# The head, the router and the tail of a two-layer decoder kernel: other load order, earlier router weights, fewer serial steps before the expert loop

## What is computed

```python
for layer in range(DEPTH):                      # 2
    h = rmsnorm(x, mix_norm[layer])
    z = h @ w_in[layer]                         # 1024 x 4392
    ...
    x = x + merged @ w_out[layer]
    h2 = rmsnorm(x, ffn_norm[layer])
    if layer % 2 == 0:
        x = x + swiglu(h2, dense_w1[i], dense_w3[i], dense_w2[i])
    else:
        x = x + moe_swiglu(h2, moe_router[i], moe_w1[i], moe_w3[i], moe_w2[i])

def moe_swiglu(h, w_router, w1, w3, w2):
    logits = einsum('bsd,de->bse', h, w_router)
    top_v, top_i = top_k(logits, 2); top_w = softmax(top_v)
    gate = sum(one_hot(top_i, 8) * top_w[..., None])
    for e in range(8):
        y = y + gate[..., e:e + 1] * swiglu(h, w1[e], w3[e], w2[e])   # hidden width 3584
```

## Time and profile before

| | us |
|---|---|
| median of 3 runs | 1618.19 (1617.88 to 1620.21) |
| the profiled execution, its own time | 1617.99 |
| its span, first to last instruction | 1616.2 |
| PE busy | 1549.6 (96%) |
| DVE busy | 1275.5 (79%) |
| ACT busy | 1052.8 (65%) |
| DMA queue q1, share of 16 engines | 80.6% |

### The profile page before, as it was taken

How to read it: one execution, slowest core, us unless ns; L and a number is a source line. 1 busy time by engine, 2 the same in 40 slices (tenths; PEclk the granted TensorE clock), 3 DMA queues, 4 the chain that set the end, 5 groups by cost and what they waited for, 6 DMA issues and landing times.

```text
span 1616.2 us, 23222 instructions
## 1 busy us (share of the span) xinstructions
PE 1549.6 (96%) x7253; PEld 1273.0 (79%) x7253; DVE 1275.5 (79%) x1358; ACT 1052.8 (65%) x1159; POOL 3.8 (0%) x9
## 2 busy tenths in 40 slices
PE   5999999999999679999999999999999999999997
PEld 4888888788888668878877877887887887887885
DVE  4785755446876569789789789889979979988978
ACT  5556544336565437677687687777768768768766
POOL 0000000000000000000000000000000000000000
PEclk8999999999999779999999999999999999999998
DMA  7553565257553649699999999989989989989985
GB/s 286 170 177 109 184 190 187 92 192 272 166 172 113 198 142 352 204 370 368 312 352 367 350 321 371 372 294 371 371 292 367 368 299 369 372 300 370 372 304 184
DMA packets 361357, 445.34 MB, mean 276 GB/s; under 512 B 17713, under 2 KB 272729, under 8 KB 361321
## 3 DMA queue, kind: packets, MB, share of 16 engines
q1 hardware_dynamic: 360840, 442.75, 80.6%
q0 software_dynamic: 480, 2.13, 0.4%
...
## 4 chain that ended last, share of the span: by engine, by line
PE 82%; issue 4%; DVE 4%; DMA 4%; ACT 3%; SPq 2%; DVEq 0%; ACTq 0%
PE bank L736 25%; PE bank L738 25%; PE bank L737 25%; DMA w_raw<-in_moe_w 3%; PE bank L1020 2%; ACT w_hi L447 2%; PE bank L1046 2%; DVE w_lo L1111 1%; SPq L353 1%; DVE hT_lo L1483 1%; PE bank L816 1%; DMA w_raw<-in_w_in 1%; PE bank L762 1%; ACT hT_hi L727 0%; PE bank L800 0%
## 5 line engine op out<-in xcount | busy, mean ns | idle before, releaser
L1111 DVE TENSOR_TENSOR w_lo<-w_raw,w_hi 128x1024 fp32r<-128x1024 f32 (+1 forms) x448 | 781.9, 1757 | 115.9 <-ACT w_hi L447 115.2
L447 ACT ACTIVATE w_hi<-w_raw 128x1024 fp32r<-128x1024 f32 (+1 forms) x448 | 664.1, 1492 | 160.7 <-PE bank L738 146.8
L736 PE MATMUL bank<-w_hi,hT_hi 128*128 128x512 f32 (+1 forms) x1424 | 567.6, 399 | 13.2 <-DVE hT_lo L1126 9.7
L738 PE MATMUL bank<-w_hi,hT_lo 128*128 128x512 f32 (+1 forms) x1424 | 555.1, 390 | 0.0
L737 PE MATMUL bank<-w_lo,hT_hi 128*128 128x512 f32 (+1 forms) x1424 | 553.9, 389 | 0.0
L736 PEld LDWEIGHTS bank<-w_hi,hT_hi 128*128 128x128 f32 x1424 | 269.0, 189 | 69.8 <-DVE hT_lo L1126 10.3
L738 PEld LDWEIGHTS bank<-w_hi,hT_lo 128*128 128x128 f32 x1424 | 268.5, 189 | 56.2
L737 PEld LDWEIGHTS bank<-w_lo,hT_hi 128*128 128x128 f32 x1424 | 269.3, 189 | 50.5
L441 ACT ACTIVATE w_hi<-w_raw 128x2048 fp32r<-128x2048 f32 (+2 forms) x100 | 169.7, 1699 | 180.2 <-PE bank L738 168.3
L1106 DVE TENSOR_TENSOR w_lo<-w_raw,w_hi 128x2048 fp32r<-128x2048 f32 (+2 forms) x100 | 201.7, 2020 | 106.7 <-ACT w_hi L441 105.5
L736 PE MATMUL bank<-w_hi,hiddenM_hi 128*128 128x512 f32 x448 | 178.8, 399 | 1.1
...
## 6 DMA issues: line engine op xcount, KB each, us to landing
...
```

Source lines behind the costliest of these rows:

```text
L447: act.activation(whi[:, m % SLOTS, 0:n], raw8[m % 8][:, 0:n], ACT.Copy).then_inc(s_hi, 1)
L736: pe.matmul(dst, ahi, bhi, start=start, stop=False)
L738: return pe.matmul(dst, alo, bhi, start=False, stop=stop)
L1111: dve.tensor_tensor(wlo[:, m % SLOTS, 0:n], raw8[m % 8][:, 0:n], whi[:, m % SLOTS, 0:n], ALU.subtract).then_inc(s_lo, 1)
```

## The change

- **Head.** SP issues the constants before `x` and then the weight chunks at once; the seven small loads are issued by ACT, the four gain rows with a semaphore of their own (`s_gn`). PE's gain matmul moves behind `x_T`, and its result is waited for at the second column block. ACT makes `hT_hi` quarters 0 and 1, splits chunk 0, makes quarters 2 and 3, then splits chunks 1 to 3; DVE likewise.
- **Router weights** are loaded by POOL at the start and split in the head, behind `norm(0)`.
- **Router.** PE takes the 48 router matmuls quarter by quarter as `hT_lo` appears, right behind `x_T(3, 1)`. `xs` is gone: ACT makes `xrhi` from `X` with the rms factor as scale, DVE makes `xrlo` in one instruction, now behind the masks. POOL clears `yhi`, `ylo` and `selT`, waited for behind `gather(0)`. `s_pos` is signalled after three matmuls. The gates move behind `gathered_lo(0)`, the overflow table is made in one pass over wider tiles. The split of the loop's fourth chunk (`ahead(c + 25)` in layer 1) moves on ACT behind `xrhi` and on DVE behind `gathered_lo(0)`.
- **Loads of the expert loop.** Chunk 7 waits for `s_ms` (norm(3)'s mean square) and not for `xrlo`.
- **Tail.** The output is stored in two DMAs of 0.5 MB, each after two of the last four `add_rows`.

The expert loop's own code is the same. SBUF addresses behind `norm_stats` shift, since the router weights have a place of their own.

```diff
+            sp.dma_start(cst[:], A["consts"]).then_inc(s_cst, 16)
             sp.dma_start(X[:], A["x"][0].rearrange("(t p) d -> p t d", p=P)).then_inc(s_x, 16)
-            sp.dma_start(cst[:], A["consts"]).then_inc(s_cst, 16)
-            for name, r, n in (("mix_norm", 0, 16), ("ffn_norm", 16, 16), ("pool_scale", 32, 8)):
-                sp.dma_start(prow[r:r + n, :], A[name].rearrange("l (k p) -> (l k) p", p=P)).then_inc(s_par, 16)
-            for j, name in enumerate(("q_norm", "k_norm")):
-                v = nrow[:].rearrange("o (l j d) -> o l j d", l=2, j=2)
-                for l in range(2):
-                    sp.dma_start(v[:, l, j], A[name][l:l + 1, :]).then_inc(s_par, 16)
...
                 elif m == 7:
-                    sp.wait_ge(s_xrl, 2)
+                    sp.wait_ge(s_ms, 4)
...
-            sp.wait_ge(m_xa, njobs * 4 + 4)
-            sp.dma_start(out[0].rearrange("(t p) d -> p t d", p=P), X[:]).then_inc(s_out, 16)
-            sp.wait_ge(s_out, 16)
+            for t in range(TT):
+                sp.wait_ge(m_xa, njobs * 4 + (2 * t + 2))
+                sp.dma_start(out[0, t * P:t * P + P, :], X[:, t, :]).then_inc(s_out, 16)
+            sp.wait_ge(s_out, 16 * TT)
...
+                if l == 0:
+                    pool.dma_start(wr[:], A["moe_router"][0].rearrange("(k p) e -> p k e", p=P)).then_inc(s_wrl, 16)
+            pool.wait_ge(s_rt, 1)
+            for z in (yhi, ylo, selT[:]):
+                ins = pool.memset(z.bitcast(F32), 0.0)
+            ins.then_inc(s_y0, 1)
 
 
         @block.scalar
...
-                ahead(c + 25)
+                if l == 0:
+                    ahead(c + 25)
                 hT_hi(3 * l + 2, 16 + 8 * l, (2, 3))
                 norm(2 * l + 1)
...
-            for c in range(LOOK):
+            for name, r, n in (("mix_norm", 0, 16), ("ffn_norm", 16, 16), ("pool_scale", 32, 8)):
+                act.dma_start(prow[r:r + n, :], A[name].rearrange("l (k p) -> (l k) p", p=P)).then_inc(s_par, 16)
+            for j, name in enumerate(("q_norm", "k_norm")):
+                v = nrow[:].rearrange("o (l j d) -> o l j d", l=2, j=2)
+                for l in range(2):
+                    act.dma_start(v[:, l, j], A[name][l:l + 1, :]).then_inc(s_gn, 16)
+            act.wait_ge(s_pcol, 1)
+            hT_hi(0, 0, (0, 1))
+            split(0, chunk_words(0))
+            hT_hi(0, 0, (2, 3))
+            for c in range(1, LOOK):
                 split(c, chunk_words(c))
-            act.wait_ge(s_x, 16)
-            act.wait_ge(s_pcol, 1)
-            hT_hi(0, 0)
             norm(0)
+            act.wait_ge(s_wrl, 16)
+            act.activation(wrhi[:], wr[:], ACT.Copy).then_inc(s_wrh, 1)
...
-            act.wait_ge(s_xs, TT)
+            act.wait_ge(s_rs, 4)
             for t in range(TT):
-                act.activation(xrhi[:, t, :], xs[:, t, :], ACT.Copy).then_inc(s_xr, 1)
+                act.activation(xrhi[:, t, :], X[:, t, :], ACT.Copy, scale=st[:, 3, t:t + 1]).then_inc(s_xr, 1)
+            ahead(LAYER1 + MIX_CHUNKS - 1)
             act.activation(identR[:], ident, ACT.Copy)
-            act.wait_ge(s_wrl, 16)
-            act.activation(wrhi[:], wr[:], ACT.Copy).then_inc(s_wrh, 1)
-            act.wait_ge(s_gd, 1)
-            act.activation(pr[:, 1, :], pr[:, 0, :], ACT.Exp).then_inc(s_ge, 1)
 
...
             gathered_hi(0)
+            act.wait_ge(s_gd, 1)
+            act.activation(pr[:, 1, :], pr[:, 0, :], ACT.Exp).then_inc(s_ge, 1)
...
-            pe.wait_ge(s_par, 7 * 16)
-            pe.transpose(bank[6][:, 0:40], prow[:], cst[0:40, C_ID:C_ID + 40])
-            pe.matmul(bank[7][:, 0:4 * HD], cst[0:1, C_ONE:C_ONE + P], nrow[:], start=True, stop=True).then_inc(s_prt, 1)
+            pe.wait_ge(s_par, 3 * 16)
+            pe.transpose(bank[6][:, 0:40], prow[:], cst[0:40, C_ID:C_ID + 40]).then_inc(s_prt, 1)
             pe.wait_ge(s_x, 16)
             x_T(0, 0)
             x_T(0, 1)
+            pe.wait_ge(s_gn, 4 * 16)
+            pe.matmul(bank[7][:, 0:4 * HD], cst[0:1, C_ONE:C_ONE + P], nrow[:], start=True, stop=True).then_inc(s_prt, 1)
             layer(0, 0)
 
...
-            pe.wait_ge(s_tlo, 24)
 
 
             pe.wait_ge(s_wrh, 2)
-            for t in range(TT):
-                for k in range(KC):
-                    ins = three(bank[4][:, t * E:t * E + E], hThi[:, k, t * P:t * P + P], hTlo[:, k, t * P:t * P + P],
-                                wrhi[:, k, :], wrlo[:, k, :], k == 0, k == KC - 1)
+            for j in range(4):
+                pe.wait_ge(s_tlo, 20 + j + 1)
+                for k in (2 * j, 2 * j + 1):
+                    for t in range(TT):
+                        ins = three(bank[4 + t][:, 0:E], hThi[:, k, t * P:t * P + P], hTlo[:, k, t * P:t * P + P],
+                                    wrhi[:, k, :], wrlo[:, k, :], k == 0, k == KC - 1)
             ins.then_inc(s_rt, 1)
             pe.wait_ge(s_mk, 1)
             tri, ones = cst[:, C_TRI:C_TRI + P], cst[:, C_ONE:C_ONE + P]
-            pe.matmul(bank[5][:, 0:E], tri, tmp8[:, 0, :], start=True, stop=True)
-            pe.matmul(bank[5][:, E:2 * E], tri, tmp8[:, 1, :], start=True, stop=False)
-            pe.matmul(bank[5][:, E:2 * E], ones, tmp8[:, 0, :], start=False, stop=True)
-            pe.matmul(bank[5][:, 2 * E:3 * E], ones, tmp8[:, 0, :], start=True, stop=False)
-            pe.matmul(bank[5][:, 2 * E:3 * E], ones, tmp8[:, 1, :], start=False, stop=True).then_inc(s_pos, 1)
+            pe.matmul(bank[6][:, 0:E], tri, tmp8[:, 0, :], start=True, stop=True)
+            pe.matmul(bank[6][:, E:2 * E], tri, tmp8[:, 1, :], start=True, stop=False)
+            pe.matmul(bank[6][:, E:2 * E], ones, tmp8[:, 0, :], start=False, stop=True).then_inc(s_pos, 1)
+            pe.matmul(bank[7][:, 0:E], ones, tmp8[:, 0, :], start=True, stop=False)
+            pe.matmul(bank[7][:, 0:E], ones, tmp8[:, 1, :], start=False, stop=True).then_inc(s_pos, 1)
...
             pe.wait_ge(s_xrl, 2)
+            gather(0)
             pe.wait_ge(s_y0, 1)
-            gather(0)
...
+            dve.wait_ge(s_pcol, 1)
+            hT_lo(0, 0, (0, 1))
+            split(0, chunk_words(0))
+            hT_lo(0, 0, (2, 3))
+            split(1, chunk_words(1))
+            dve.wait_ge(s_prt, 2)
             dve.tensor_copy(gain[:].rearrange("p l j d -> p (l j d)"), bank[7][:, 0:4 * HD]).then_inc(s_pcol, 1)
-            for c in range(LOOK):
+            for c in range(2, LOOK):
                 split(c, chunk_words(c))
             dve.wait_ge(s_pcol, 2)
-            hT_lo(0, 0)
             norm(0)
+            dve.wait_ge(s_wrh, 1)
+            dve.tensor_tensor(wrlo[:], wr[:], wrhi[:], ALU.subtract).then_inc(s_wrh, 1)
...
-                dve.tensor_scalar(xs[:, t, :], X[:, t, :], st[:, 3, t:t + 1], None, ALU.mult).then_inc(s_xs, 1)
-            dve.wait_ge(s_xs, TT)
+                ins = dve.tensor_scalar(lg[:, t, :], bank[4 + t][:, 0:E], st[:, 3, t:t + 1], None, ALU.mult)
+            chain(ins)
             for t in range(TT):
-                dve.wait_ge(s_xr, t + 1)
-                dve.tensor_tensor(xrlo[:, t, :], xs[:, t, :], xrhi[:, t, :], ALU.subtract).then_inc(s_xrl, 1)
-            dve.wait_ge(s_wrh, 1)
-            dve.tensor_tensor(wrlo[:], wr[:], wrhi[:], ALU.subtract).then_inc(s_wrh, 1)
-            dve.wait_ge(s_rt, 1)
-            for z in (yhi, ylo, selT[:]):
-                ins = dve.memset(z.bitcast(F32), 0.0)
-            ins.then_inc(s_y0, 1)
+                ins = dve.max(v8[:, t, :], lg[:, t, :])
+            chain(ins)
             for t in range(TT):
-                chain(dve.tensor_scalar(lg[:, t, :], bank[4][:, t * E:t * E + E], st[:, 3, t:t + 1], None, ALU.mult))
-            for t in range(TT):
-                chain(dve.max(v8[:, t, :], lg[:, t, :]))
-            for t in range(TT):
-                chain(dve.max_index(ix8[:, t, :], v8[:, t, :], lg[:, t, :]))
-            dve.tensor_tensor(pr[:, 0, :], v8[:, :, 1], v8[:, :, 0], ALU.subtract).then_inc(s_gd, 1)
+                ins = dve.max_index(ix8[:, t, :], v8[:, t, :], lg[:, t, :])
+            chain(ins)
             chain(dve.tensor_copy(ixf[:], ix8[:]))
             iota8 = cst[:, C_IOTA:C_IOTA + E]
             for t in range(TT):
                 dve.tensor_scalar(m0[:, t, :], iota8, ixf[:, t, 0:1], None, ALU.is_equal)
-                chain(dve.tensor_scalar(m1[:, t, :], iota8, ixf[:, t, 1:2], None, ALU.is_equal))
+                ins = dve.tensor_scalar(m1[:, t, :], iota8, ixf[:, t, 1:2], None, ALU.is_equal)
+            chain(ins)
             chain(dve.tensor_tensor(tmp8[:], m0[:], m1[:], ALU.add))
             dve.nop().then_inc(s_mk, 1)
-            dve.wait_ge(s_ge, 1)
-            chain(dve.tensor_scalar(pr[:, 2, :], pr[:, 1, :], 1.0, None, ALU.add))
-            chain(dve.reciprocal(pr[:, 2, :], pr[:, 2, :]))
-            chain(dve.tensor_tensor(pr[:, 3, :], pr[:, 1, :], pr[:, 2, :], ALU.mult))
             for t in range(TT):
```

(23 more changed lines are left out.)

55 lines of the change are left out of this document (39 added, 16 removed).

## The result

The changed kernel takes 1593.23 us (median, runs from 1591.34 to 1593.62), the kernel before beside it 1619.14 us. The ratio is 0.984, with a 95% interval from 0.9828 to 0.9852. The profiled execution took 1593.62 us with a span of 1591.8; that of before 1617.99 with 1616.2. The forecast of 1591.3 is 1.9 us low, inside its range; the gain was forecast at 26.9 us and is 25.9 by the medians.

The account below looks back on a forecast made before the run. PE, busy 96% of the span, was taken to bound the kernel. Savings of 10.2 (head), 15.5 (router) and 1.2 us (tail), 26.9 in all, turned the median 1618.19 into 1591.3 us, range 1585 to 1597.

Parts of the forecast that it names:

- Step (a): Head: `x`, now issued behind the constants, lands at 8.0 us, 3.3 us ahead of the earlier first `x_T`.
- (d): Head: ACT splits chunk 0 from 11.14, DVE from 12.36 to 13.75, `hT_lo` 0 and 1 ahead; PE starts at 13.8.
- Step (c): Head: chunk 0's split still begins on landing at 11.14 us, up to 1 us sooner if small loads held the queue.
- Step (b): Head: `hT_hi` quarters 0 and 1 are ready at 10.7 us; ACT's DMA issues and table load end near 5.5.
- rival B: Head keeps only part, through a new layer 0 wait or late `x`: 4 to 6 us lost, 1595 to 1597; chance 0.12.
- the masks 8.6 us ahead: Router: expected sign that the masks come 8.6 us ahead of their earlier distance from 545.6 us, the end of layer 1.
- rival C: Router: POOL's clearing slows DVE's logits and masks, 2.4 us more, 1593.7, or 1596 if `xrlo` doubles too; chance 0.09.
- row and rule: Router clock: the profile row shows 0.50 under packed matmuls; the skill's rule says PE activity keeps it up. Row taken.
- rival A: Router: the clock stays up, 3.1 us more gained, 1588.2; with gather and first products too, 1583.3; chance 0.20.
- Rival E: An early quarter still waits for something late, such as router weights; PE's 11 us wait stays, 1602; chance 0.04.
- Rival D: Expert loop loses its weight feed, stalling longer every job; at 5 us a job, 1631, slower than before; chance 0.03.
- the slack: Expert loop: DMA needs only 118 us a job against PE's 127, so it catches up by 8 us a job.

Follow-up runs that it names:

- the two exchanges: The kernel before with only the change's head: 1608.97 us; the changed kernel with the head of before: 1602.61 us.
- the kernel with `early`: Changed kernel plus a small early ACT instruction writing an added tile: 1621.57 us; with wide matmuls in waits, head and router too: 1617.24 us.

## Why the prediction was right, and where its terms were off

The working held term by term. Of the 26.9 us it summed, 24.4 are in the profiled execution: head -1.0, layer 0 -0.54, router +0.65, loop -1.8, tail +0.19.

**Head, 10.2, measured 9.2 in the trace and 10.0 and 9.7 in the two exchanges.** Step (a) holds: `x` is there at 8.0. So does the order in (d), 1.0 us later. Step (c) was mis-sized: chunk 0 lands at 11.7 to 12.1 (its split waits for the DMA until then in the three kernels with the early table load) and not at 11.14. I had expected at most a gain there, and had named a landing past 12 as a sign of being wrong. Why it lands later isn't shown: the seven small loads on ACT's queue move only 0.02 MB. Step (b) failed in one point: the table load "end near 5.5" in fact stood behind the wait of ACT's first activation and ran from 9.22 to 10.50. It cost 0.4 us at most, as chunk 0 was hardly earlier. Layer 0 gave back 0.54 us: 23 products, 0.25 us apart, ran at the lower clock instead of 19, 5.7 us instead of 4.7. A new wait in layer 0, rival B's mechanism, isn't there; only its other half occurred, `x` late. It lands between 7.6 and 8.0 in nine profiled executions and at 9.22, 10.73 and 11.26 in three, with the same load order, so the hit at 8.0 was luck in part; the execution with 11.26 took 3.3 us more than the median of its kernel, that with 10.73 took 3.4.

**Router, 15.5, measured 16.15.** Twenty-four matmuls ran at the upper level instead of 18, which is 0.5 of the 1.0 us by which the logits came sooner than the forecast by distance; the rest is an earlier start beside the end of `x_T` and DVE's shorter delay. That it was 24 is luck: with the same router it was 9 to 26. (Of 10.66 us for 48 matmuls each would have 0.222; the 0.213 is the distance of starts. The sign "the masks 8.6 us ahead" doesn't follow from the sum, which gives 572.35 - 556.8 = 15.6; it was 16.1.) Masks took 2.88 us instead of 2.4, for the cast beside POOL: rival C, with 0.65 us where it had put 2.4. Positions to gather took 1.24 instead of 1.35, and gather to product 9.55 us where it said 9.54. The choice between row and rule was right: the clock fell under packed matmuls, in this execution and in the eight others, and rival A didn't occur. Rival E didn't either, since the first router matmul waits for nothing; the kernel with late weights shows what it would have looked like.

**Tail, 1.2, measured 1.39.**

**The loop, costed at nothing, took back 1.8 us in one profile and 0.6 in the other.** The prediction had read that the first products run with the lower clock, and took the stretch as fixed. It isn't: the clock came back 5.8 us after the first product. At half the rate the 2.9 us more are worth 1.4, close to the 1.1 to 1.3 that job 0 is longer, and the five lengths of job 0 beside the fourth chunk's split rise with this delay. What wide matmuls bring in job 0 is the same effect turned round.

**Rival D** didn't occur: a chunk less in the ring cost nothing that shows in job 0, and the three router tiles that moved ahead of the ring's second half (768 bytes) left its rates as they were. What it feared, the DMAs behind PE in every job, came in the kernel with `early` by another route, slower DMAs: 3.9 us in each of seven jobs, 27.6 us in all, against the 26.9 from which it decides. And the slack was overrated. I had set 44 MB against the page's best slice, 118 us. By the changed kernel's rates four of seven groups of w1 and w3 chunks come at 348 GB/s and three at 385, and w2 at 403: 117 us, and each job has a dip besides. With `early`, 348 and 387 make 122, and the dip adds the rest of the 131, some 9 us. If the changed kernel's dip needs as much, an estimate of 1 us of the 8 that I had counted as slack was there.
